# Gate and up projections by one Strassen step: seven half-block products, gone through product by product over a group of pairs

## The chip, the cores and the metric

The kernel runs on one core of one Trainium2 chip. The metric is the device time of one execution in microseconds. Engines are named PE (TensorE), DVE (VectorE), ACT (ScalarE), POOL (GpSimd) and SP (SyncE, which issues most DMAs).

## The reference, cut to what matters

The model is a two-layer decoder trunk over 1088 tokens (1024 prompt tokens and 64 sample tokens), width 1024, hidden width 2816, all in float32. Each layer has an attention part and then this feed-forward part; only the feed-forward part is changed.

```
def rms_norm(x, g):
    y = x * lax.rsqrt(jnp.mean(x * x, axis=-1, keepdims=True) + EPS)
    return y * g

def swiglu(x, w_gu, w_dn):
    gate, up = jnp.split(x @ w_gu, 2, axis=-1)      # w_gu: 1024 x 5632
    return (jax.nn.silu(gate) * up) @ w_dn          # w_dn: 2816 x 1024

xp = xp + swiglu(rms_norm(xp, g_ffn[l]), w_gate_up[l], w_down[l])
```

## The kernel before, in words

Everything is kept transposed: features on the 128 partitions, the 1088 tokens along the free axis. The width 1024 is 8 blocks of 128 rows. To get float32 accuracy from the fast float32r matmul, every operand is split into a rounded part ("high", `WH`, `XH`) and the rest ("low", `WL`, `XL`), and a product is three passes: high by high, high by low, low by high. The high part is a copy on ACT, the low part a subtraction on DVE.

A weight matrix comes in slabs of 128 output columns. One slab (`slab`, L1478) is 8 row blocks times 3 passes times 3 column chunks of 384, 384 and 320 tokens (`CH`), 72 matmuls, accumulated in three banks of the on-chip accumulator PSUM. Two slabs are in flight (`j` = 0 and 1): banks 0 to 2 and banks 3 to 5.

The hidden width is 22 blocks of 128. They are gone through in four groups of 6, 6, 5 and 5 (`FCH`, L44). For each group, the phase `gu` runs pairs of slabs, first the gate slab, then the up slab of the same hidden block; then the phase `dn` multiplies the group's hidden blocks by their rows of `w_down`, in 8 slabs, and adds to the residual `XT`. The order on every engine is written out by hand (`t_phase` on ACT L641, DVE L981, PE L1494; `ffn` on ACT L816, DVE L1221, PE L1765), with counting semaphores between engines; PE's phases are hardware loops.

Per gate/up slab the stations are: SP loads 512 KB into one half of `RAW` (L355, once the former slab's high and low parts are made), POOL multiplies it by the norm's gain (`scale`, L488 to L499), ACT makes `WH` (`split_hi`, L630 to L639), DVE makes `WL` (`split_lo`, L976 to L979), PE multiplies. Per pair, DVE multiplies the gate's sums by the reciprocal root mean square `RB` into `GT`, ACT applies silu, DVE multiplies by `RB` again (L1234), then by the up sums from PSUM (L1239); ACT makes the high part `HH` (L828), DVE the low part `HL` (L1242). POOL does nothing else in the feed-forward part. At the start of a layer's feed-forward part, `after_o` (L669, L1204) makes `XH` and `XL` of the residual, `sums` (L1511) sums squares with a matmul by ones, and `roots` and `rstd` turn them to `RB`.

`copies` (L233) sends two DRAM-to-DRAM copies of 2032 KB each (the cache outputs) down SP's queue, once in each of the eight groups, after the group's fourth gate/up slab.

## Time and profile before

| | |
|---|---|
| time, median of 3 runs | 2522.32 us (2521.43 to 2523.72) |
| profiled execution, first to last instruction | 2520.1 us; its time outside this span is not recorded |
| PE matmul busy | 2429.5 us, 96% |
| DVE / ACT / POOL busy | 999.8 (40%) / 673.0 (27%) / 373.8 us (15%) |
| mean granted PE clock | 0.989 of full |
| DMA | 186.65 MB, mean 74 GB/s |
| first feed-forward part | about 409 to 1172 us from the span's start |
| second feed-forward part | about 1724 to 2496 us |

In the slices of the page (40 of 63 us each) PE stands at 9 tenths in nearly all; the exceptions are the attention part of the first layer (slices 1 to 4), that of the second (slices 22 to 27), and the end. In the feed-forward slices DVE is at 2 to 3 tenths, ACT at 1, POOL at 1 or 0.

### The profile page before, as it was taken

Reading aid. Unit: us, or ns where it says so; the run is one execution under the profiler, and the core shown is the slowest. Engines: PE = TensorE matmul, PEld = TensorE weight load, DVE = VectorE, ACT = ScalarE, POOL = GpSimd, SP = SyncE. Lnnn points to the kernel's source line nnn. Section 1 sums busy time; section 2 is a strip of 40 time slices with the busy share of each in tenths; the row PEclk is TensorE's granted clock in tenths of the full one; section 3 lists DMA queues with packets and bytes.
Section 4 is the critical chain, followed back from the end, with each engine's and each line's share of the span. In section 5 each row is a group of like instructions: output and inputs, shape, how many; then the busy total and the mean of one; then the engine's idle time right before and its main releaser. Section 6 shows DMA issues by size and latency. Waiting matters only on the chain. (4 is left out here: it accounts for less than half of the span.)

```text
span 2520.1 us, 40445 instructions
## 1 busy us (share of the span) xinstructions
PE 2429.5 (96%) x16347; PEld 2343.7 (93%) x16347; DVE 999.8 (40%) x1883; ACT 673.0 (27%) x1283; POOL 373.8 (15%) x282
## 2 busy tenths in 40 slices
PE   8999899999999999999999998789999999999997
PEld 7888699999999999999999976489999999999997
DVE  6466535332322332335312377556322332232235
ACT  4345424211111111113110187443311110111123
POOL 2333201101100100101111110511101100101100
PEclk9999999999999999999999999899999999999998
DMA  4010214113111311311121234713113111312212
GB/s 176 21 54 20 87 51 133 48 37 113 50 35 48 116 33 51 108 38 54 63 85 49 72 92 138 263 53 113 47 38 114 44 40 50 108 38 67 95 35 87
DMA packets 64939, 186.65 MB, mean 74 GB/s; under 512 B 11288, under 2 KB 17816, under 8 KB 64056
## 3 DMA queue, kind: packets, MB, share of 16 engines
q1 hardware_dynamic: 63928, 180.46, 22.0%
q0 software_dynamic: 912, 4.85, 0.5%
q8 instruction: 65, 1.06, 0.2%
q14 instruction: 34, 0.28, 0.0%
HBM read 175.85 MB, written 44.70 MB: 88 GB/s over the span
## 5 line engine op out<-in xcount | busy, mean ns | idle before, releaser
L978 DVE TENSOR_TENSOR WL<-RAW,WH 128x1024 fp32r<-128x1024 f32 (+3 forms) x196 | 220.0, 1124 | 1137.3 <-ACT WH L639 1136.6
L1488 PE MATMUL PS<-XH,WH 128*128 128x384 f32 x2640 | 582.5, 328 | 2.8 <-DVE XL L1005 1.6
L1488 PE MATMUL PS<-XL,WH 128*128 128x384 f32 x2640 | 581.7, 328 | 0.0
L1488 PE MATMUL PS<-XH,WL 128*128 128x384 f32 x2640 | 581.7, 328 | 0.0
L639 ACT CAST WH<-RAW 128x1024 fp32r<-128x1024 f32 (+3 forms) x196 | 184.8, 944 | 1154.0 <-PE PS L1488 1137.7
L498 POOL TENSOR_TENSOR RAW<-RAW,GAIN 128x1024 f32<-128x1024 f32 x112 | 217.1, 1940 | 1636.9 <-DMA RAW<-in_w_gu 1383.0
L1488 PEld LDWEIGHTS PS<-XH,WH 128*128 128x128 f32 x2640 | 450.5, 188 | 3.9 <-DVE XL L1005 1.9
L1488 PEld LDWEIGHTS PS<-XH,WL 128*128 128x128 f32 x2640 | 450.6, 188 | 0.0
L1488 PEld LDWEIGHTS PS<-XL,WH 128*128 128x128 f32 x2640 | 450.6, 188 | 0.0
L1488 PE MATMUL PS<-HL,WH 128*128 128x384 f32 (+1 forms) x1041 | 228.7, 327 | 0.0
L1488 PE MATMUL PS<-HH,WL 128*128 128x384 f32 (+1 forms) x1041 | 228.5, 327 | 0.0
L1488 PE MATMUL PS<-HH,WH 128*128 128x384 f32 (+1 forms) x1041 | 228.5, 327 | 0.0
L1488 PEld LDWEIGHTS PS<-HH,WL 128*128 128x128 f32 x1041 | 176.0, 188 | 0.0
L1488 PEld LDWEIGHTS PS<-HH,WH 128*128 128x128 f32 x1041 | 176.0, 188 | 0.0
L1488 PEld LDWEIGHTS PS<-HL,WH 128*128 128x128 f32 x1041 | 175.9, 188 | 0.0
L1188 DVE TENSOR_TENSOR XT<-XT,PS 128x768 f32 (+3 forms) x158 | 106.2, 713 | 3.5 <-PE PS L1488 3.4
L537 POOL TENSOR_TENSOR SA<-SA,SM 128x512 f32<-128x512 f32 (+1 forms) x64 | 72.3, 1131 | 129.3 <-DVE SM L1104 129.3
L732 ACT ACTIVATE SA<-SA,SM 128x257 f32<-128x257 f32 (+1 forms) x128 | 62.6, 491 | 99.8 <-DVE SM L1095 99.8
L857 ACT ACTIVATE SB<-SB,ST 128x128 f32<-128x128 f32 (+1 forms) x192 | 84.3, 446 | 8.8 <-DVE ST L1287 8.8
L1242 DVE TENSOR_TENSOR HL<-HT,HH 128x1088 f32 (+1 forms) x44 | 56.9, 1292 | 59.0 <-ACT HH L828 59.0
L828 ACT CAST HH<-HT 128x1088 f32 (+1 forms) x44 | 48.6, 1104 | 112.9 <-DVE HT L1239 112.9
L1234 DVE TENSOR_TENSOR GT<-GT,RB 128x1088 f32<-128x1088 f32 x44 | 56.9, 1292 | 52.0 <-ACT GT L824 52.0
(235 smaller groups left out, 2443.5 us busy)
## 6 DMA issues: line engine op xcount, KB each, us to landing
RAW<-in_w_gu SPq DMA_DIRECT2D x88, 512.0 KB, 3.6
out_bkS<-in_bk_in SPq DMA_DIRECT2D x8, 2032.0 KB
out_bvS<-in_bv_in SPq DMA_DIRECT2D x8, 2032.0 KB
RAW<-in_w_dn SPq DMA_DIRECT2D x32, 384.0 KB, 3.0
KC<-in_bk_in SPq DMA_DIRECT2D x8, 1536.0 KB, 11.5
VC<-in_bv_in SPq DMA_DIRECT2D x8, 1536.0 KB, 6.9
RAW<-in_w_dn SPq DMA_DIRECT2D x32, 320.0 KB, 2.9
XT<-in_xT SPq DMA_DIRECT2D x16, 544.0 KB, 5.4
```

Of the source, the lines that this page charges most:

```text
L498: nc.gpsimd.tensor_tensor(w, w, g, ALU.mult).then_inc(S["scaled"], 1)
L537: nc.gpsimd.tensor_tensor(p, p, SM[:, 24 + 2 * b:26 + 2 * b].unsqueeze(2).to_broadcast([P, 2, w]), ALU.mult).then_inc(S["a_norm"], 1)
L639: nc.scalar.copy(to[:, j, 0:nk * P], RAW[:, j, 0:nk * P]).then_inc(S["wh"], 1)
L732: ins = nc.scalar.activation(SA[:, b, kk, 256 - w:257], SA[:, b, kk, 256 - w:257], ACT.Exp, bias=SM[:, h:h + 1], scale=-1.0, accum_out=SM[ ...
L828: nc.scalar.copy(HH[:, ds(i * TOK, TOK)], HT[:]).then_inc(S["hh"], 1)
L857: ins = nc.scalar.activation(s, s, ACT.Exp, bias=ST[:, g, blk, 2 * p + kk:2 * p + kk + 1], scale=-1.0, accum_out=ST[:, g, blk, 8 + 2 * p + ...
L978: nc.vector.tensor_tensor(lo[:, j, 0:nk * P], RAW[:, j, 0:nk * P], hi[:, j, 0:nk * P].bitcast(F32), ALU.subtract).then_inc(S["wl"], 1)
L1188: ins = nc.vector.tensor_tensor(x, x, ps, ALU.add)
L1234: nc.vector.tensor_tensor(GT[:], GT[:], RB[:], ALU.mult).then_inc(S["gt"], 1)
L1242: nc.vector.tensor_tensor(HL[:, ds(i * TOK, TOK)], HT[:], HH[:, ds(i * TOK, TOK)].bitcast(F32), ALU.subtract).then_inc(S["hx"], 1)
L1488: ins = mm(PS[:, 3 * j + c, 0:width], w[:, j, k * P:(k + 1) * P], x(k, a, width), start=(k == 0 and n == 0), stop=(k == nk - 1 and n == 2))
```

## The change: what it does

The block matrix product is done by Strassen's scheme once. Tokens are cut into two halves of 544, the width 1024 into two halves of 4 blocks, and the output columns of a pair into gate and up. With X(ij) the half blocks of the activations (i: rows 0 to 3 or 4 to 7 of the width, j: token half) and W the four quarter slabs of a pair (gate or up, upper or lower rows), seven products of half size replace eight. A product is 4 row blocks times 3 passes times 2 chunks of 272 tokens, 24 matmuls, in two PSUM banks.

In each group of n pairs the program goes through product 0 for all n pairs, then product 1, and so on: seven phases of n products ("g" counts them, 0 to 7n-1, phase = g // n). What each phase needs and leaves, beside its matmuls:

| phase | weights summed on POOL | activations summed on POOL | PSUM copies on ACT | PSUM adds on DVE |
|---|---|---|---|---|
| 0 | yes | no | 2 | 0 |
| 1 | no | yes | 1 | 1 |
| 2 | yes | no | 1 | 1 |
| 3 | no | yes | 0 | 2 |
| 4 | yes | yes | 0 | 2 |
| 5 | yes | yes | 0 | 1 |
| 6 | yes | yes | 0 | 1 |

The results are accumulated in on-chip memory: `GA` and `UA`, two halves of 544 for each pair. The sums of activations go to `TS` in four pieces per phase, and their high and low parts to `TH` and `TL` (double buffered by phase). The gain is now multiplied into the activations by ACT (`gained`, into `XG`), so POOL's `scale` over the gate/up weights goes. The weight ring has four places instead of two. Both multiplications of the gate by `RB` move from DVE to POOL (`gate_rms`), before and after silu: one half of the tokens during phases 3 and 4, the other during phases 5 and 6. The product with up, and `HH` and `HL`, are made per token half (`hidden`, `hidden_low`), in phases 5 and 6 and just behind. The down projection keeps its matmuls. Most of the diff is the bookkeeping of semaphore counts and buffers; below is its core, first the constants, then POOL's functions, DVE's `ffn` and PE's `product`. The loops over the feed-forward part are written out; the cache copies are issued at the second slab of the down phase.

```diff
 FCH = (6, 6, 5, 5)
+HALF = TOK // 2
+CHK = HALF // 2
+NPH = 7
+PAIRED = (0, 2, 4, 5, 6)
+SUMMED = (1, 3, 4, 5, 6)
+COPIES = (2, 1, 1, 0, 0, 0, 0)
+ADDS = (0, 1, 1, 2, 2, 1, 1)
...
+            def weight_sum(l, c, g):
...
+                pool.wait_ge(S[f"raw{r}"], 16 * n)
+                one, two = ring(r)[:, 0:4 * P], ring(r)[:, 4 * P:KT * P]
+                if ph < 5:
+                    ins = nc.gpsimd.tensor_tensor(one, one, two, ALU.add)
...
+            def operand_sum(l, c, ph, k):
...
+                pool.wait_ge(S["slab"], operand_free(l, c, ph))
...
+                nc.gpsimd.tensor_tensor(TS[operand_slot(l, c, ph)][:, k * HALF:(k + 1) * HALF], one, two, op).then_inc(S["ts"], 1)
+            def gate_rms(l, c, i, h, again):
...
+                    pool.wait_ge(S["gad"], evicted(ADDS, l, c, (5, 3)[h] * FCH[c] + i))
...
+                nc.gpsimd.tensor_tensor(g, g, RB[:, h * HALF:(h + 1) * HALF], ALU.mult).then_inc(S[f"g{h + 1}{'m' if again else 'r'}"], 1)
+            def ffn(l):
+                for g in range(4):
+                    weight_sum(l, 0, g)
+                for c, n in enumerate(FCH):
+                    for g in range(NPH * n):
+                        ph, i = divmod(g, n)
+                        for h, at in ((1, 3), (0, 5)):
+                            if 0 <= g - 3 - at * n < n:
+                                gate_rms(l, c, g - 3 - at * n, h, True)
+                        if g + 4 < NPH * n:
+                            weight_sum(l, c, g + 4)
+                        for h, at in ((1, 3), (0, 5)):
+                            if 0 <= g - 2 - at * n < n:
+                                gate_rms(l, c, g - 2 - at * n, h, False)
+                        if i < 4 and ph + 1 in SUMMED and (ph or c == 0):
+                            operand_sum(l, c, ph + 1, i)
+                    if c + 1 < len(FCH):
+                        for k in range(4):
+                            operand_sum(l, c + 1, 1, k)
+                        for g in range(4):
+                            weight_sum(l, c + 1, g)
...
             def ffn(l):
...
+                    for g in range(NPH * n):
+                        ph, i = divmod(g, n)
+                        if g:
+                            product_adds(l, c, g - 1)
...
+                        if g + 3 < NPH * n:
+                            gate_up_low(l, c, g + 3)
...
+                        if 0 <= g - 1 - 6 * n:
+                            hidden(l, c, g - 1 - 6 * n, 1)
+                        if 1 <= i < 5 and ph + 1 < NPH and (ph or c == 0):
+                            operand_low(l, c, ph + 1, i - 1)
...
+                        if 0 <= g - 4 - 5 * n < n:
+                            hidden(l, c, g - 4 - 5 * n, 0)
+                        if 0 <= g - 5 - 5 * n < n:
+                            hidden_low(l, c, g - 5 - 5 * n, 0)
+                        if 0 <= g - 2 - 6 * n:
+                            hidden_low(l, c, g - 2 - 6 * n, 1)
+                    product_adds(l, c, NPH * n - 1)
+                    hidden(l, c, n - 1, 1)
+                    hidden_low(l, c, n - 2, 1)
+                    hidden_low(l, c, n - 1, 1)
...
+            def product(l, c, g):
...
+                pe.wait_ge(S["wl"], PLAN.first[f"gu{l}{c}"] + g + 1)
+                if g >= 3:
+                    pe.wait_ge(S["gcp"], evicted(COPIES, l, c, g - 3))
+                    if evicted(ADDS, l, c, g - 3):
+                        pe.wait_ge(S["gad"], evicted(ADDS, l, c, g - 3))
...
+                for k in range(4):
+                    if i == 0:
+                        pe.wait_ge(S["tl"], piece(l, c, ph, k))
+                    for n, (w, x) in enumerate(((wh, TH[q]), (wh, TL[q]), (wl, TH[q]))):
+                        for d in range(2):
+                            a = k * HALF + d * CHK
+                            ins = mm(PS[:, b + d, 0:CHK], w[:, k * P:(k + 1) * P], x[:, a:a + CHK],
+                                     start=(k == 0 and n == 0), stop=(k == 3 and n == 2))
```

## Rows read from the trace of the kernel before

**Rows 1.** The page: span, and part 1, busy us of each engine.
```profile
span 2520.1 us, 40445 instructions
PE 2429.5 (96%) x16347; PEld 2343.7 (93%) x16347; DVE 999.8 (40%) x1883; ACT 673.0 (27%) x1283; POOL 373.8 (15%) x282
```
**Rows 2.** Windows over the feed-forward parts: length, busy of each engine, clock, DMA, GB/s.
```profile
409.00:937.00 528.00, 528.00 (x3175) 527.92 (x3174) 163.58 (x179) 96.54 (x93) 59.36 (x31) 1.00 0.22 70
...
1724.00:2496.00 772.00, 772.00 (x4643) 771.93 (x4642) 243.13 (x276) 144.55 (x142) 76.31 (x40) 1.00 0.19 60
```
**Rows 3.** PE's waits, the longest: us in total, times, longest.
```profile
PE PS L1862 <- ACT CB L914: 19.3, 7, 4.2
```
**Rows 4.** Timeline of PE in a gate/up slab: start us, us, instruction, count.
```profile
702.16 0.66 PE L1488 MATMUL PS<-XH,WL 128*128 128x384 f32 x3
...
706.66 0.66 PE L1488 MATMUL PS<-XH,WL 128*128 128x384 f32 x3
```
**Rows 5.** The line of 256-column matmuls: ns min/median/max, first and last start.
```profile
L1538 PE MATMUL PS<-WHV,XH x72: 279/281/357, 42.0 to 67.5; 128*128 128x256 f32 x72
...
L1538 PE MATMUL PS<-WLV,XH x72: 274/281/285, 42.2 to 67.7; 128*128 128x256 f32 x72
```
**Rows 6.** DVE groups by shape: count, busy us, mean ns, idle before.
```profile
L1234 DVE TENSOR_TENSOR GT<-GT,RB 128x1088 f32<-128x1088 f32 x44 | 56.9, 1292 | 52.0 <-ACT GT L824 52.0
L1188 DVE TENSOR_TENSOR XT<-XT,PS 128x768 f32 x52 | 49.2, 947 | 0.0
L978 DVE TENSOR_TENSOR WL<-RAW,WH 128x640 fp32r<-128x640 f32 x32 | 26.4, 825 | 161.0 <-ACT WH L639 161.0
L1188 DVE TENSOR_TENSOR XT<-XT,PS 128x320 f32 x52 | 25.0, 480 | 0.0
L1023 DVE RECIPROCAL RB<-RB 128x384 f32<-128x384 f32 x8 | 19.9, 2524 | 10.0 <-ACT RB L684 10.0
```
**Rows 7.** One line of DVE, four instructions of 512 columns: ns min/median/max.
```profile
L1035 DVE TENSOR_TENSOR WL<-RAW,WH x4: 679/691/1522, 5.7 to 15.1; 128x512 fp32r<-128x512 f32 x4
```
**Rows 8.** POOL groups by shape.
```profile
L537 POOL TENSOR_TENSOR SA<-SA,SM 128x512 f32<-128x512 f32 x56 | 67.2, 1202 | 100.4 <-DVE SM L1104 100.3
L587 POOL TENSOR_TENSOR QB<-QB 128x512 f32<-128x512 f32 x16 | 24.5, 1534 | 33.5 <-DVE QB L1357 30.9 <-issue 2.2 <-POOL SQN L578 0.2
L594 POOL TENSOR_TENSOR PSB<-PSB 128x256 f32<-128x256 f32 x8 | 5.8, 727 | 9.8 <-ACT PSB L881 9.3
L596 POOL TENSOR_TENSOR PSB<-PSB 128x64 f32<-128x64 f32 x8 | 2.5, 318 | 0.0
```
**Rows 9.** Timeline of DVE from 1193 us.
```profile
1193.45 1.29 DVE L1017 TENSOR_TENSOR SQS<-SQS,SQ 128x1088 f32<-128x1088 f32 x1
1194.65 2.99 DVE L1005 TENSOR_TENSOR XL<-XT,XH 128x1088 fp32r<-128x1088 f32 x1
```
**Rows 10.** Timeline of POOL in the same stretch.
```profile
1193.68 2.82 POOL L498 TENSOR_TENSOR RAW<-RAW,GAIN 128x1024 f32<-128x1024 f32 x1 [5.49 <-DMA RAW<-in_w_kB]
```
**Rows 11.** Timelines of DVE and of POOL at 99.5 us.
```profile
99.54 0.47 DVE L1095 CUSTOM_DVE_ANT_0 SA<-PS,TABA,NSINK 128x256 f32<-128x256 f32 x1
...
98.56 1.04 POOL L537 TENSOR_TENSOR SA<-SA,SM 128x512 f32<-128x512 f32 x1 [1.70 <-DVE SM L1104]
99.56 1.90 POOL L520 TENSOR_TENSOR RAW<-RAW,GAIN 128x1024 f32<-128x1024 f32 x1
```
**Rows 12.** ACT group of the weight copies of 512 columns.
```profile
L639 ACT CAST WH<-RAW 128x512 fp32r<-128x512 f32 x8 | 4.9, 620 | 10.9 <-PE PS L1488 10.8
```
**Rows 13.** Windows over two attention stretches, columns as in Rows 2.
```profile
1580.00:1660.00 80.00, 60.43 (x888) 39.20 (x886) 45.53 (x100) 38.83 (x88) 41.97 (x59) 0.84 0.56 199
280.00:290.00 10.00, 7.42 (x126) 5.87 (x122) 5.17 (x17) 6.59 (x16) 2.04 (x2) 1.00 0.19 57
```
**Rows 14.** SP's queue at the first cache copies, and DMA issues with us to landing.
```profile
408.23 15.65 SPq L239 DMA_DIRECT2D out_avS<-in_av_in  x1
RAW<-in_w_gu SPq DMA_DIRECT2D x88, 512.0 KB, 3.6
```

More of the change, by code:

```diff
@@ L75, in __init__ @@
             self.scaled[name] = z
-            z += n if name[:2] not in ("oA", "oB", "dn") else 0
-            g += 0 if name[0] == "v" else n // 2
+            z += n if name[:2] not in ("oA", "oB", "dn", "gu") else 0
+            g += 0 if name[0] == "v" or name[:2] == "gu" else n // 2
+            self.raw[name] = tuple(raw[:2])
+            if name[:2] in ("gu", "dn"):
+                first = self.first[f"gu{name[2]}0"]
+                for x in range(n):
+                    r = (self.first[name] + x - first) % 4
+                    raw[r] += 2 if name[:2] == "gu" and x * NPH // n == 4 else 1
+                    self.ring[name, x] = r, raw[r]
+            else:
+                raw[0] += n // 2
+                raw[1] += n // 2
     def end(self, name):
@@ L542, in _ @@
                     scale_one("qA", 4 + U // 8, 0)
-            for c in range(len(FCH)):
-                scale(f"gu0{c}", 1)
+            def weight_sum(l, c, g):
+                ph = g // FCH[c]
+                if ph not in PAIRED:
+                    return
+                r, n = PLAN.ring[f"gu{l}{c}", g]
+                pool.wait_ge(S[f"raw{r}"], 16 * n)
+                one, two = ring(r)[:, 0:4 * P], ring(r)[:, 4 * P:KT * P]
+                if ph < 5:
+                    ins = nc.gpsimd.tensor_tensor(one, one, two, ALU.add)
+                elif ph == 5:
+                    ins = nc.gpsimd.tensor_tensor(one, one, two, ALU.subtract)
+                else:
+                    ins = nc.gpsimd.tensor_tensor(one, two, one, ALU.subtract)
+                ins.then_inc(S["gsum"], 1)
@@ L647, in pair @@
                             split_hi(name, 2 * i + j + 2, j)
-                        elif prefetch and PLAN.next(name) and not (j and name == "oA"):
+                        elif ahead and j == 0:
+                            ahead()
+                        elif prefetch and PLAN.next(name) and not ahead:
                             split_hi(PLAN.next(name), j, j)
@@ L801, in evac @@
                     k = 2 * i + j
-                    if not split and isinstance(k, int) and k == KT - 1:
+                    if norm in (1, 4) and isinstance(k, int) and k == KT - 1:
                         return
@@ new lines, in down_low, with first_jobs, ahead @@
+            def down_low(l, c, x):
+                r, _ = PLAN.ring[f"dn{l}{c}", x]
+                dve.wait_ge(S["wh"], PLAN.first[f"dn{l}{c}"] + x + 1)
+                nc.vector.tensor_tensor(down_slot(WL, c, x), ring(r)[:, 0:FCH[c] * P], down_slot(WH, c, x).bitcast(F32),
+                                        ALU.subtract).then_inc(S["wl"], 1)
+            def first_jobs(l):
+                def ahead():
+                    if l:
+                        for k in range(4):
+                            operand_low(l, 0, 0, k)
+                    for g in range(2):
+                        gate_up_low(l, 0, g)
+                return ahead
@@ new lines, in down @@
+            def down(l, c, x):
+                n, b = FCH[c], down_bank(c, x)
+                pe.wait_ge(S["wl"], PLAN.first[f"dn{l}{c}"] + x + 1)
+                if x < 2:
+                    pe.wait_ge(S["gad"], evicted(ADDS, l, c, NPH * n - 2 + x))
+                else:
+                    pe.wait_ge(S[f"free{x % 2}"], PLAN.groups[f"dn{l}{c}"] + x // 2)
+                wh, wl = down_slot(WH, c, x), down_slot(WL, c, x)
+                for k in range(n):
+                    if x == 0:
+                        pe.wait_ge(S["hl1"], pairs_ahead(l, c) + k + 1)
+                        pe.wait_ge(S["hl2"], pairs_ahead(l, c) + k + 1)
+                    for m, (w, h) in enumerate(((wh, HH), (wh, HL), (wl, HH))):
+                        for d, (a, width) in enumerate(CH):
+                            ins = mm(PS[:, b + d, 0:width], w[:, k * P:(k + 1) * P], h[:, k * TOK + a:k * TOK + a + width],
+                                     start=(k == 0 and m == 0), stop=(k == n - 1 and m == 2))
+                ins.then_inc(S["slab"], 1)
@@ L1771, in _ @@
+            def ffn(l):
+                for c, n in enumerate(FCH):
+                    for g in range(NPH * n):
+                        product(l, c, g)
+                        if c == 0 and g == n:
+                            norm_sums(1 + 2 * l, (0, 1))
+                        if c == 0 and g == n + 2:
+                            norm_sums(1 + 2 * l, (2,))
+                    for x in range(KT - 1 if (l, c) == (1, len(FCH) - 1) else KT):
+                        down(l, c, x)
             ffn(0)
```

463 lines of the change are left out of this document (356 added, 107 removed).

## The prediction

> **What bounds the kernel now.** I read the page's busy times first: PE is busy 96% of a span of 2520.1 us, no other engine over 40% [rows 1]. Then windows over the feed-forward parts, to see whether the idle 4% lies there: it does not. In 528, 235 and 772 us PE is busy in every microsecond at full granted clock (1.00, the level of 2.4 GHz), DVE 31 to 34% and POOL 9 to 11% of the time [rows 2]. The list of PE's waits agrees: the longest, 19.3 us, stands on a line of the attention part [rows 3]. So the part that changes is bound by PE alone, and two things decide: how much PE work goes, and whether the work that Strassen hands to the lightly used DVE and POOL still fits beside what is left.
>
> **PE's side.** Before, a pass over one row block is three matmuls, 1088 columns; nine passes after 702.16 us the same pass starts at 706.66: 4.50 / 9 = 0.500 us [rows 4], 166.7 ns a matmul of 363 columns. A pair takes 2 x 8 x 3 x 0.500 = 24.0 us, a group of 5 pairs 120 us, of 6 pairs 144 us. After, a pair is 7 x 24 = 168 matmuls of 272 columns. No row has that width. The nearest has 256: 216 matmuls start between 42.0 and 67.7 us, 25.7 / 215 = 119.5 ns each [rows 5]. Interpolated to 272 with the slope to 363 columns, (166.7 - 119.5) / 107 = 0.44 ns a column, it is 126.5 ns; bounds are 119.5 and 141.7 ns (three quarters of 166.7 by columns would be 125, plus one whole 16.7 ns if all of the width step were fixed cost). A product is then 24 x 0.1265 = 3.04 us, a pair 21.3 us, a group 106.3 (n=5) or 127.5 us (n=6). If PE remained the bound, 4 x (13.7 + 16.5) = 121 us would go.
>
> **The others' side.** Prices. DVE with both inputs in on-chip memory: 1292 ns for 1088 columns, 825 for 640 [rows 6], 679 to 691 for 512 when undisturbed [rows 7]; so 0.69 us for a weight low (512 columns), 0.725 for 544 columns (operand low, hidden, hidden low). DVE with one input in PSUM: 947 at 768, 480 at 320 [rows 6], so 0.71 us for 544. POOL with two full inputs: 727 ns at 256 columns and 318 at 64 [rows 8], a slope of 2.13 ns a column: 1.27 us for a weight sum (512), 1.34 for 544 columns (operand sum, gate_rms). The bounds for 512 columns are 1.04 us (the 1202 ns row, whose second input is two values repeated; 1.04 is its undisturbed time, as its first timeline entries show and 1202 is with waits) and 1.53 us (the strided adds of L587) [rows 8]. I take 1.27, since it comes from contiguous operands like these.
>
> The price that decides is another: DVE and POOL exclude each other. At 1193.68 POOL is given a scaling of 1.90 us while DVE is in a subtraction (end 1194.74); it ends at 1196.50, so it began only when DVE was through. DVE's next operation, issued at 1194.65, takes 2.99 us instead of 1.28 and ends 1.14 us behind POOL's end [rows 9, 10]. One POOL and one DVE operation thus take 2.99 us where their own times add to 3.18: strictly one after the other, less 0.19 us of overlap at the change. An operation of DVE that reads PSUM is not held: 0.47 us as usual under a running POOL multiplication [rows 11]. So product_adds run freely, but every weight low, operand low, hidden and hidden low shares one resource with every POOL operation; I call it the shared path.
>
> Now count the shared path by phase, from the loops in the diff (n=5, a group that is not a layer's first):
>
> - phase 0: DVE 6, POOL 1: 5.4 us; phase 1: 9 and 4: 11.4 us; phase 2: 9 and 5: 13.0 us. PE needs 15.2 us for each, and DVE's adds (5 x 0.71) run beside POOL: PE stays the bound, 45.6 us in all.
> - phase 3: DVE 5 weight lows, 4 operand lows, 6.4 us; POOL 4 weight sums, 5 gate_rms, 4 operand sums, 17.1 us: 23.5 us.
> - phase 4: DVE 6.4; POOL 5 + 5 + 4, 18.4: 24.8 us.
> - phase 5: DVE 7.1; POOL 5 + 5 + 4, 18.4: 25.5 us.
> - phase 6 with its tail: DVE 2 weight lows, 1 down low (0.82), 19 hidden operations, 16.0; POOL 1 + 5, 8.0: 24.0 us.
>
> Phases 3 to 6: 97.7 us on the shared path against 4 x 15.2 = 60.8 us on PE. For n=6 the same count gives 26.9 + 26.7 + 31.6 + 27.5 = 112.7 us against 73.0; phases 0 to 2 take PE's 54.7.
>
> From these I take off the overlaps at the changes: 34 alternations (the smaller count of each phase) x 0.19 and 1.7 us for back-to-back operations, 97.7 - 8.5 = 89.2 us; for n=6, 40 x 0.19 and 1.8: 112.7 - 9.8 = 102.9 us (with no overlap at all, 97.7 and 112.7, the high bound).
>
> Can the queues shift work out of phases 3 to 6? POOL is in order: operand sums of phase ph+1 wait until PE is through phase ph-1, gate_rms waits for DVE's adds of two products ago, and the weight sums stand between them. The 29 us that the shared path idles in phases 0 to 2 cannot be used. PE can only be some 3 products ahead (its banks wait for the adds of product g-3). Forward, the tail can overlap: the first down slab takes its hidden blocks one by one, 1.5 us each (nine matmuls), so I take off 3 us for hidden operations beside PE; and add 1.5 us in phase 6, where POOL runs out of work before DVE and DVE's five adds of 0.71 no longer hide. Net 1.5 us off; bounds 0 and 6 off.
>
> Group of 5: 45.6 + 89.2 - 1.5 = 133.3 us against 120: +13.3. Group of 6: 54.7 + 102.9 - 1.5 = 156.1 against 144: +12.1. Four of each: +101.6 us.
>
> **The remaining edits.** ACT per product: a weight high 0.62 us [rows 12], up to two PSUM copies of about that, pieces of 544 at half of 1115 ns plus start; under 2 us of 3.04, hidden. The norm's reciprocals (7 us of DVE, phase 1 of a layer's first group) fit: DVE has 18.2 us there for 11.4 of its own. That group also gets its phase-1 operand sums and lows in phase 0, 8.3 us on top of 7.4 in 18.2: fits. A layer's start needs 4 operand pieces instead of 8: -3 to +5 us, taken as 0. Each product now loads up to 512 KB; a load lands in 3.6 us [rows 14] with four ring places, about seven products ahead: hidden. The cache copies keep SP busy for 15.65 us [rows 14] and now stand ahead of the third down slab's load, issued some six products before the down phase; that slab is needed 6 x 3.04 + 15 = 33 us later: hidden; if not, up to 10 us in each of eight groups.
>
> **Rule against row.** The only two-input POOL rows are short or strided. The Trainium skill (GPSIMD Engine Reference, section 3.1) puts a two-input elementwise operation at about 2.6 cycles an element at 1.2 GHz, since both operands come through one port; that would be 1.11 us plus dispatch for 512 columns, nearer 1.27 than 1.04, and speaks against the change: the sum by it is the one above, by the cheap row it would be the third case below.
>
> **Sum.** 2520.1 + 101.6 = 2621.7 us of span. The median lies 2.2 us above the span, so 2624 us.
>
> **Rivals.**
> (a) Forecast: shared path binds phases 3 to 6. Own range 2580 to 2690 (no overlap: +70 us; 6 us off: -36 us).
> (b) Faster: PE stays the bound because POOL and DVE together stay under 3.04 us a product. Price: 121 us off, 2401 us, perhaps 2410 with starts. It decides where the shared path of phases 3 to 6 is below 60.8 us (n=5). For it: DVE at 33% and POOL at 10% now, ring and banks several deep. Against it: POOL's own 62 us in those phases already exceed 60.8 even if DVE were never in the way. Chance 0.13.
> (c) POOL runs at the cheap price, 1.04 and 1.11 us: 10.8 us less (n=5), 12.5 (n=6), 93 in all: 2531 us. For it the repeated-operand rows, against it the 727/318 pair. Chance 0.12.
> (d) Dearer: PE idles about a third of phases 3 to 6, and its clock may fall. With 76% busy it was granted 0.84 on average, a mix of the 1.2 and 2.4 GHz levels, but 1.00 with 74% elsewhere [rows 13]. A product at 1.2 GHz takes 24 x 272 / 1200 + 0.32 = 5.76 us; all of phases 3 to 6 so: 115 against 89, 138 against 103, in all +245: 2869. A mean clock of 0.84 still carries 68% busy, so the forecast has 0 for it. The strided POOL price gives +114, 2738. Chance 0.17.
> (a) keeps 0.58.
>
> **Numbers.** Range 2500 to 2740: leaves out (b), and the far end of (d). What can be told from no change is about 0.2%, 5 us. Faster 0.17 ((b) and the low part of (c)), within 0.04, slower 0.79.
>
> **What would show it.** After: POOL busy near 900 us instead of 374, with mean durations of its 544-column operations well above 1.34 and DVE's two-input ones above 0.73, while the PSUM adds stay at 0.71. Windows by phase: PE at 100% in phases 0 to 2 and the down phases, near 70% in phases 3 to 6, n products taking 22 to 26 us. Products in phases 0 to 2 at 3.04 us show the matmul price. It would be wrong if POOL and DVE ran side by side, if the matmul pitch at 272 columns were over 135 ns, or if PE's waits in these parts were for loads or PSUM copies instead of WL, TL and HL.

## The result and the profile after

The changed kernel takes 2682.39 us (median of 4 runs, 2681.75 to 2683.32), the kernel before 2523.02 us (2521.43 to 2524.16) beside it: ratio 1.0635, 95% interval 1.0622 to 1.0648. It is 6.35% slower. The profiled execution of the changed kernel has a span of 2680.5 us, 160.4 us more than before [rows 1], at a mean granted clock of 0.954 of full.

The page of the changed kernel, span and busy us of each engine:

```profile
span 2680.5 us, 43596 instructions
PE 2390.0 (89%) x17403; PEld 2285.7 (85%) x17403; DVE 1599.0 (60%) x2575; ACT 969.6 (36%) x1973; POOL 1088.5 (41%) x750
```

PE is recorded busy for 39.5 us less than before [rows 1], not for the 121 us less that were forecast: part of its work now runs at a fallen clock and takes longer (in x1 below, at a mean granted clock of 0.987, the same matmuls keep it busy for 2302.9 us, 127 us less than before). It stands idle for 290 us instead of 91. DVE went from 1000 to 1599 us, POOL from 374 to 1088: these are recorded durations, and the next rows show that they hold waiting. The groups of POOL and of DVE in the changed kernel (count, then busy us, mean ns of one, then idle time before them):

```profile
L726 POOL TENSOR_TENSOR GA<-GA,RB 128x544 f32<-128x544 f32 x176 | 287.5, 1635 | 44.7 <-ACT GA L1082 44.7
L715 POOL TENSOR_TENSOR TS<-XG 128x544 f32<-128x544 f32 x160 | 255.5, 1608 | 125.0 <-PE PS L2197 119.4 <-ACT XG L879 5.6
L700 POOL TENSOR_TENSOR RAW<-RAW 128x512 f32<-128x512 f32 x66 | 97.2, 1473 | 389.1 <-DMA RAW<-in_w_gu 389.1
```
```profile
L1519 DVE TENSOR_TENSOR TL<-TS,TH 128x544 fp32r<-128x544 f32 x160 | 222.1, 1388 | 5.2 <-ACT TH L893 1.8
L1583 DVE TENSOR_TENSOR UA<-UA,GA 128x544 f32<-128x544 f32 x88 | 109.1, 1262 | 2.5
L1576 DVE TENSOR_TENSOR UA<-UA,PS 128x544 f32<-128x544 f32 x88 | 62.2, 707 | 0.0
```

An operand low takes 1388 ns on average where it needs 720, a product with up 1262. The addition with an input in PSUM, of the same 544 columns, stays at 707 ns. That is the picture of rows 9 to 11, now in every group: who reads two operands from on-chip memory takes turns with POOL, who reads PSUM does not.

PE's waits in the changed kernel, the longest (us in total, times, longest):

```profile
PE PS L2197 <- DVE UA L1576: 76.7, 45, 3.0
PE PS L2197 <- DVE TL L1519: 43.2, 23, 3.7
PE PS L2216 <- issue: 27.2, 4, 7.1
PE PS L2216 <- DVE WL L1531: 26.1, 4, 7.7
PE PS L2197 <- DVE GA L1574: 23.3, 12, 4.1
PE PS L2321 <- ACT CB L1220: 19.3, 7, 4.2
```

Before, the longest was the last of these [rows 3]; now five stand ahead of it, 196.5 us, all in the feed-forward part. Three are the products' (L2197), for DVE's additions and lows; two are the first down slab's (L2216). None is a load or a copy by ACT. The largest part, 100.0 us, is for the additions from PSUM (L1576 and L1574). They are not slower than before, they come late: DVE works through its queue in order, and they stand in it behind operations that POOL holds up.

Windows over the second group of 6 pairs in the first layer (phases 0 to 2, phases 3 to 6, the down phase) and over its last group of 5 (phases 0 to 2, phases 3 to 6; columns as in rows 2: length, busy of PE, PE's weight loads, DVE, ACT, POOL, then granted clock, DMA share, GB/s):

```profile
636.50:690.50 54.00, 54.00 (x433) 54.00 (x432) 30.36 (x40) 27.83 (x50) 14.69 (x10) 1.00 0.39 118
690.70:798.70 108.00, 79.99 (x579) 77.09 (x577) 91.61 (x90) 34.40 (x57) 93.67 (x58) 0.94 0.45 145
798.70:872.20 73.50, 73.50 (x432) 73.50 (x433) 26.28 (x37) 12.57 (x19) 6.88 (x6) 0.97 0.18 56
1071.60:1116.60 45.00, 45.00 (x361) 45.00 (x361) 24.16 (x35) 23.93 (x43) 12.77 (x9) 1.00 0.40 124
1116.70:1204.90 88.20, 67.75 (x482) 65.81 (x480) 71.41 (x75) 29.61 (x49) 75.84 (x47) 0.91 0.46 146
```

In phases 0 to 2 PE is busy in every microsecond at full clock, 54.0 and 45.0 us. In phases 3 to 6 PE's 72 and 60 us of matmuls take 108.0 and 88.2. DVE and POOL are each recorded busy for 81 to 87% of that stretch; where one of DVE's instructions with both inputs in on-chip memory or one of POOL's is under way (the union of their records, worked out from the trace) it is 102.4 of 108.0 and 84.2 of 88.2 us.

Where the 160.4 us lie, from the first matmuls of each phase in the trace. Eight groups, four of each size:

| stretch | PE's minimum forecast | forecast | measured |
|---|---|---|---|
| phases 0 to 2 | 401 | 401 | 396.8, and 6.6 more in phase 0 of the two first groups |
| phases 3 to 6, n=5 | 243 | 351 | 360.7 (92.1, 88.3, 92.0, 88.3) |
| phases 3 to 6, n=6 | 292 | 406 | 432.4 (108.2, 108.0, 108.2, 108.0) |
| gate and up, sum (before: 1056) | 936 | 1158 | 1196.5 |
| down phases, over before | 0 | 0 | +17.4 (+1.9 to +2.4 each) |
| all else | 0 | 0 | +2.5 |

1196.5 - 1056 + 17.4 + 2.5 = 160.4 us. The sums of squares by PE in the first groups (two matmul groups, about 2 us a layer) are in both kernels and left out of the rows.

### The profile page after: what moved, and what is told of

Read it like the earlier page. It is cut to its first block and busy times, and to the rows that moved or that the text cites. A ratio compares the mean times of both kernels' runs of the same rounds, so it can differ in the third digit from the quotient of the medians.

```text
span 2680.5 us, 43596 instructions
## 1 busy us (share of the span) xinstructions
PE 2390.0 (89%) x17403; PEld 2285.7 (85%) x17403; DVE 1599.0 (60%) x2575; ACT 969.6 (36%) x1973; POOL 1088.5 (41%) x750
## 5 line engine op out<-in xcount | busy, mean ns | idle before, releaser
L2197 PE MATMUL PS<-TH,WH 128*128 128x272 f32 x2464 | 538.1, 301 | 149.4 <-DVE UA L1576 76.7
L2197 PEld LDWEIGHTS PS<-TH,WH 128*128 128x128 f32 x2464 | 406.3, 198 | 167.8 <-issue 115.4
L2197 PE MATMUL PS<-TH,WL 128*128 128x272 f32 x2464 | 527.8, 297 | 0.0
L2197 PE MATMUL PS<-TL,WH 128*128 128x272 f32 x2464 | 525.5, 296 | 0.0
L2197 PEld LDWEIGHTS PS<-TL,WH 128*128 128x128 f32 x2464 | 405.1, 197 | 0.0
L2197 PEld LDWEIGHTS PS<-TH,WL 128*128 128x128 f32 x2464 | 402.9, 197 | 0.0
L715 POOL TENSOR_TENSOR TS<-XG 128x544 f32<-128x544 f32 x160 | 255.5, 1608 | 125.0 <-PE PS L2197 119.4
L726 POOL TENSOR_TENSOR GA<-GA,RB 128x544 f32<-128x544 f32 x176 | 287.5, 1635 | 44.7 <-ACT GA L1082 44.7
L2216 PE MATMUL PS<-HH,WH 128*128 128x384 f32 (+1 forms) x1041 | 236.9, 337 | 53.3 <-issue 27.2
L2216 PE MATMUL PS<-HL,WH 128*128 128x384 f32 (+1 forms) x1041 | 234.7, 334 | 0.0
L2216 PE MATMUL PS<-HH,WL 128*128 128x384 f32 (+1 forms) x1041 | 232.6, 332 | 0.0
L2216 PEld LDWEIGHTS PS<-HH,WH 128*128 128x128 f32 x1041 | 181.7, 194 | 54.9 <-issue 27.9
L1519 DVE TENSOR_TENSOR TL<-TS,TH 128x544 fp32r<-128x544 f32 x160 | 222.1, 1388 | 5.2 <-ACT TH L893 1.8
L1525 DVE TENSOR_TENSOR WL<-RAW,WH 128x512 fp32r<-128x512 f32 x156 | 140.5, 904 | 108.0 <-ACT WH L903 107.9
L2216 PEld LDWEIGHTS PS<-HL,WH 128*128 128x128 f32 x1041 | 182.2, 194 | 0.0
L2216 PEld LDWEIGHTS PS<-HH,WL 128*128 128x128 f32 x1041 | 180.1, 192 | 0.0
L646 POOL TENSOR_TENSOR RAW<-RAW,GAIN 128x1024 f32<-128x1024 f32 x24 | 58.6, 2447 | 215.9 <-DMA RAW<-in_w_qB 89.8
```

The costliest lines, as they stand in the source:

```text
L646: nc.gpsimd.tensor_tensor(w, w, g, ALU.mult).then_inc(S["scaled"], 1)
L715: nc.gpsimd.tensor_tensor(TS[operand_slot(l, c, ph)][:, k * HALF:(k + 1) * HALF], one, two, op).then_inc(S["ts"], 1)
L726: nc.gpsimd.tensor_tensor(g, g, RB[:, h * HALF:(h + 1) * HALF], ALU.mult).then_inc(S[f"g{h + 1}{'m' if again else 'r'}"], 1)
L1519: nc.vector.tensor_tensor(TL[q][:, a:b], x, TH[q][:, a:b].bitcast(F32), ALU.subtract).then_inc(S["tl"], 1)
L1525: nc.vector.tensor_tensor(slot(WL, c, g), ring(r)[:, 0:4 * P], slot(WH, c, g).bitcast(F32), ALU.subtract).then_inc(S["wl"], 1)
L2197: ins = mm(PS[:, b + d, 0:CHK], w[:, k * P:(k + 1) * P], x[:, a:a + CHK], start=(k == 0 and n == 0), stop=(k == 3 and n == 2))
```

## The experiments

Each run is compared with runs of the kernel before on the same chip. The medians of the kernel before on these chips are 2521.6 to 2524.5 us, so some 3 us between two runs from different chips mean nothing. x1 and x2 ran once, the others four or five times. Theory A is that of the prediction: the shared path of DVE and POOL bounds phases 3 to 6. The letters B to H are its rivals, as each expectation states them.

### x1_pool_stub: POOL's work in the feed-forward part cut to one column

```diff
-                one, two = ring(r)[:, 0:4 * P], ring(r)[:, 4 * P:KT * P]
+                one, two = ring(r)[:, 0:1], ring(r)[:, 4 * P:4 * P + 1]
...
-                nc.gpsimd.tensor_tensor(g, g, RB[:, h * HALF:(h + 1) * HALF], ALU.mult)
+                nc.gpsimd.tensor_tensor(g[:, 0:1], g[:, 0:1], RB[:, h * HALF:h * HALF + 1], ALU.mult)
```

The operand sums are cut in the same way, and the lows read `XG` instead of their result.

> The changed kernel with every POOL operation of the feed-forward parts (weight sums, operand sums, both gate multiplications) cut to one column, all waits and all work of the other engines kept; so the sums are left out of the result. Theory A (DVE's two-input operations and POOL's operations take turns on one shared path, and that path bounds phases 3 to 6): with POOL's 70 to 85 us a group gone, PE is the bound except at the tail, where DVE's own 19 hidden operations and the adds of phase 6 (about 19 us against 15) still stand over; groups of about 108 (n=5) and 129 us (n=6), the whole 2420 to 2450 us. DVE's 544-column two-input operations go back to 0.72 us from 1.26 to 1.39. Rival B (DVE is late by itself, or loads and PSUM copies are late): DVE keeps its work, so at least half of the 160 us stays, 2600 us or more. Rival C (the granted clock of PE does it): clock returns to 0.99 with the idle gone, so C alone doesn't part from A here.

Measured: 2403.27 us (one run), against 2524.45 before. A group takes 128 to 131 and 106 us, PE's own 126.3 and 105.3, the down phases are back at 71.6 (one: 73.1) and 59.7 to 59.9. All instructions of all engines are still there (43596). The groups of DVE in this kernel:

```profile
L1519 DVE TENSOR_TENSOR TL<-XG,TH 128x544 fp32r<-128x544 f32 x224 | 160.1, 719 | 6.7 <-ACT TH L893 6.7
L1525 DVE TENSOR_TENSOR WL<-RAW,WH 128x512 fp32r<-128x512 f32 x156 | 106.7, 687 | 60.1 <-ACT WH L903 60.1
...
L1576 DVE TENSOR_TENSOR UA<-UA,PS 128x544 f32<-128x544 f32 x88 | 62.9, 714 | 0.0
L1583 DVE TENSOR_TENSOR UA<-UA,GA 128x544 f32<-128x544 f32 x88 | 61.4, 721 | 2.5
```

The operand low falls from 1388 to 719 ns, the product with up from 1262 to 721, the PSUM addition stays. So the columns that POOL works on account for 2682.4 - 2403.3 = 279 us, and with them gone the change brings the 121 us that PE alone was forecast to save: nothing else in it (waits, copies, loads, turnover of banks) costs PE more than the 2 us at the end of a group of 6. It is the time of rival (b), 2401 us, and 17 us under the lower end expected here; why A's estimate was that much too high was not looked into. x1 alone does not say whether POOL's columns cost by holding DVE or by POOL's own queue being full; x5 does.

### x2_rms_stub: only the gate's multiplications cut to one column

```diff
-                nc.gpsimd.tensor_tensor(g, g, RB[:, h * HALF:(h + 1) * HALF], ALU.mult)
+                nc.gpsimd.tensor_tensor(g[:, 0:1], g[:, 0:1], RB[:, h * HALF:h * HALF + 1], ALU.mult)
```

> The changed kernel with only the two gate multiplications on POOL cut to one column (the gate is not normalised in the result). Theory A: 20 (n=5) or 24 (n=6) operations of 1.34 us leave the shared path of phases 3 to 6, which falls to about 65 and 74 us against PE's 60 and 72; with 3 us of tail a group takes about 114 and 132 us, the whole about 2480 to 2505 us, some 180 to 200 us less than the changed kernel. Rival B (DVE alone, its operations and adds, or the loads): under 40 us less.

Measured: 2492.06 us (one run), in A's range. 176 multiplications of 1.35 us are 238 us; leaving them out gives 190 us. Groups go from 162.1 to 137.1 (the second) and from 133.4 to 111.4 us (the last): phases 4 and 5 now run at PE's 18.0 and 15.0 to 15.6, and only phase 6 is late (28.9 and 20.6). The multiplications are the largest part, but what is left of POOL's work still delays phase 6, which takes 20.1 and 15.6 us in x1.

### x3_late_sums: the next group's operand sums wait for the down phase

```diff
                     if c + 1 < len(FCH):
+                        pool.wait_ge(S["slab"], PLAN.first[f"dn{l}{c}"] + 1)
                         for k in range(4):
                             operand_sum(l, c + 1, 1, k)
```

> The changed kernel, complete, with one more wait on POOL: the four operand sums for the next group (and the weight sums behind them) start only when the first down slab is through, not when the last product is. In the trace these four POOL operations alternate with DVE's last three hidden operations, which the first down slab waits for. Theory A: they cost what the last group of each layer, which has no such sums, does without: 137.1 - 133.4 = 3.7 us in each of six groups, so 18 to 26 us less than the changed kernel. Rival D (the tail is bound by the chain DVE, ACT, DVE alone): no change, within 4 us.

Measured: 2654.76 us (2653.61 to 2657.49), ratio 1.0523 (1.0505 to 1.0540), 27.6 us less than the changed kernel. Behind phase 6 the changed kernel's POOL starts the four sums of the next group at once, and three of DVE's last hidden operations (the product with up, L1583, and its low, L1589) alternate with them. The first down slab does not wait for these three themselves, as the expectation has it, but for what stands behind them in DVE's queue: here the addition that ends at 2194.92. The changed kernel, POOL, then DVE, then PE's first matmul of the down phase:

```profile
2179.48 1.35 POOL L726 TENSOR_TENSOR GA<-GA,RB 128x544 f32<-128x544 f32 x1 [1.89 <-ACT GA L1082]
2188.56 6.92 POOL L715 TENSOR_TENSOR TS<-XG 128x544 f32<-128x544 f32 x4 [7.73 <-PE PS L2197]
```
```profile
2182.58 1.35 DVE L1589 TENSOR_TENSOR HL<-UA,HH 128x544 fp32r<-128x544 f32 x2
...
2188.02 0.96 DVE L1531 TENSOR_TENSOR WL<-RAW,WH 128x768 fp32r<-128x768 f32 x1
2188.89 1.85 DVE L1583 TENSOR_TENSOR UA<-UA,GA 128x544 f32<-128x544 f32 x1
2190.67 3.62 DVE L1589 TENSOR_TENSOR HL<-UA,HH 128x544 fp32r<-128x544 f32 x2
2194.21 0.71 DVE L1576 TENSOR_TENSOR UA<-UA,PS 128x544 f32<-128x544 f32 x1
```
```profile
2195.02 1.25 PE L2216 MATMUL PS<-HH,WH 128*128 128x384 f32 x3 [6.54 <-issue]
```

The program has PE wait there until the addition of the last product but one has emptied its bank, and in all four groups of 6 the down phase starts 0.1 us behind that addition. In the groups of 5 it starts 0.1 us behind the first weight low of the down phase (L1531), which stands behind the same addition in DVE's queue.

With the sums held back, DVE in the same place of the second group:

```profile
789.64 0.72 DVE L1584 TENSOR_TENSOR UA<-UA,GA 128x544 f32<-128x544 f32 x1
790.28 1.35 DVE L1590 TENSOR_TENSOR HL<-UA,HH 128x544 fp32r<-128x544 f32 x2
```

Two lows take 1.35 us with POOL idle and 3.62 beside it. In each layer the three groups that have a successor gain 3.4 to 4.0 us each, 22 us in all, and the last one nothing (133.4 to 133.3). In the profiled executions, 28.3 us apart, the down phases give 2.7 us, and the rest lies outside the feed-forward parts, where this edit changes nothing. This is a term that the prediction did not have.

### x4_warm: eight more matmuls in each product of phases 4 to 6

```diff
+                    for e in range(8 if k == 0 and ph >= 4 else 0):
+                        mm(PS[:, b + e % 2, 0:CHK], wh[:, 0:P], TH[q][:, 0:CHK], start=True, stop=True)
```

> The changed kernel, complete, with eight more matmuls of 272 columns at the head of each product of phases 4 to 6 (overwritten by the product's first pass, so nothing changes in the result): 1.0 us of PE work in stretches where PE idles 5 to 18 us a phase. Theory A: the shared path sets the pace there, so the extra 8 x 15 to 18 us a group cost nothing; what changes is the granted clock, which fell to 1.2 GHz for 10 to 17 us in each group: part of it comes back, and with it at most the 2 us by which each down phase was longer and some of the tail, 0 to 20 us less in all (2660 to 2685). Rival C (the clock is the cause of the loss): 40 us less or more. Rival E (PE is nearly the bound in these phases): 60 to 120 us more.

Measured: 2673.88 us (2672.34 to 2678.37), ratio 1.0601 (1.0583 to 1.0618), 8 us less than the changed kernel with 1056 matmuls more. The extra ones are 1056 x 0.1253 = 132 us of PE. The same stretch as above, phases 3 to 6 of the second group, now runs at the full clock:

```profile
690.00:796.00 106.00, 91.38 (x717) 89.84 (x715) 88.76 (x89) 33.98 (x57) 91.94 (x57) 1.00 0.43 147
```

Its clock is 1.00 instead of 0.94, and phases 3 to 6 take 106.8 us instead of 108.0. Over phases 3 to 6 of all groups the granted clock stands at 0.50 for 38 us instead of 138, and yet these phases take 790.2 us instead of 793.1 in the profiled executions. So PE has slack there that 132 us of work fit into, and the fallen clock costs about 3 us there, since it falls where PE waits anyway. The other 5 of the 8 us are not traced to it: the profiled execution is the slowest of the four. At the start of the down phases the clock still falls, to 0.50 for 3.2 to 6.2 us in every group, and they take as long as in the changed kernel (535.1 and 534.6 us in all); x4 does not price that.

### x5_rms_dve: the gate's multiplications on DVE

```diff
-                nc.gpsimd.tensor_tensor(g, g, RB[:, h * HALF:(h + 1) * HALF], ALU.mult)
+                nc.vector.tensor_tensor(g, g, RB[:, h * HALF:(h + 1) * HALF], ALU.mult)
```

The calls move from POOL's loop to DVE's, behind `product_adds`, in the same order.

> The changed kernel, complete, with both gate multiplications issued by DVE at the same places of its queue instead of by POOL. Theory A: the same work stays on the shared path, but at 0.725 us each instead of 1.35, so phases 3 to 6 lose 12.3 (n=5) and 14.8 us (n=6), less some overlap: about 80 to 110 us less in all, 2575 to 2600 us. Rival F (POOL's queue alone is the bound, DVE and POOL run side by side): POOL falls from 62 to 35 us in phases 3 to 6, DVE's own 72 us minus its 9 us of overlaps is then the longest, 63 against 88 us now: 180 to 200 us less. Rival B (DVE alone is the bound): 14.5 to 17.4 us more of DVE work a group, 100 us slower.

Measured: 2622.33 us (2619.47 to 2625.93), ratio 1.0395 (1.0377 to 1.0412): 60 us less than the changed kernel. The direction is A's, and F and B fell, but A's own size, 80 to 110 us, was missed. The window over phases 3 to 6 of the second group tells why:

```profile
685.90:787.90 102.00, 80.54 (x580) 78.56 (x578) 98.74 (x114) 33.29 (x57) 56.77 (x34) 0.92 0.46 154
```

DVE is recorded busy for 98.7 of 102.0 us, POOL for 56.8, and the union of the shared instructions is 88.6. The shared path now has 13 us free, but DVE has not: it also carries the PSUM additions, and whenever POOL is in the way the whole queue of DVE stands. A reading that fits is a second bound beside the shared path: DVE's own work plus the work of POOL that it is blocked by.

### x6_norm_first: activations normalised once, no multiplication of the gate

The residual times gain (`XG`, 8 blocks of 1088 columns) is multiplied by `RB` before the first product, so that gate and up come out normalised and `gate_rms` goes. The late sums of x3 are in.

```diff
+            def normalise(l, k):
+                dve.wait_ge(S["xg"], KT * l + k + 1)
+                x = XG[:, ds(k, 1)].rearrange("p a h n -> p (a h n)")
+                nc.vector.tensor_tensor(x, x, RB[:], ALU.mult).then_inc(S["xr"], 1)
...
-                                gate_rms(l, c, g - 3 - at * n, h, True)
...
-                                gate_rms(l, c, g - 2 - at * n, h, False)
```

> A complete kernel: the changed kernel, but the activations are multiplied by the reciprocal root mean square before the first product (eight DVE operations of 1088 columns a layer), so both gate multiplications go; the sums of squares, roots and reciprocals move ahead of the first product; and the wait of the experiment with late sums is in. Theory A: phases 3 to 6 have about 65 and 74 us on the shared path against 60 and 72 on PE, groups of about 112 and 130 us, first groups without the reciprocals in them; the two layer starts now wait some 14 us each for the chain square, sum, root, three reciprocals, multiplication. In all 2520 + 8 x (121 - 132) + 28 + 7 = 2467, between 2450 and 2500 us: faster than the kernel before. Rival B (DVE bound): 2600 us or more.

Measured: 2515.17 us (2510.69 to 2519.11), ratio 0.9969 (0.9953 to 0.9984), 15 us above the expected range. The groups that do not start a layer came near what A says, 133.0 to 133.6 us (about 130 expected) and 110.8 to 112.3 (about 112). What was underrated is the layer's start. DVE there:

```profile
402.37 6.98 DVE L1313 RECIPROCAL RB<-RB 128x384 f32<-128x384 f32 x3 [2.35 <-ACT RB L906]
409.38 2.49 DVE L1534 TENSOR_TENSOR XG<-XG,RB 128x1088 f32<-128x1088 f32 x2
...
416.90 7.13 DVE L1534 TENSOR_TENSOR XG<-XG,RB 128x1088 f32<-128x1088 f32 x4
423.95 3.57 DVE L1507 TENSOR_TENSOR WL<-GR,WH 128x512 fp32r<-128x512 f32 x2
```

Three reciprocals (7.0 us) and the multiplications stand ahead of the first operand low, so the first product starts at 412.7 us instead of 394.7, and phase 0 takes 27.9 us where PE needs 18.0: 28 us in the first layer against PE's pace. Against the changed kernel, whose phases 0 and 1 take 22.0 and 19.9 us, it is 22 us. PE waits there, and it also runs slower: the mean granted clock of this phase 0 is 0.78.

### x7_norm_wdve: x6, and the weight sums of phases 5 and 6 on DVE

```diff
+            def late_weight_sum(l, c, g):
...
+                nc.vector.tensor_tensor(one, a, b, ALU.subtract).then_inc(S["gsd"], 1)
...
+                        if g + 4 < NPH * n:
+                            late_weight_sum(l, c, g + 4)
```

> A complete kernel: the one with normalised activations, with the weight sums of phases 5 and 6 (2n a group) issued by DVE four products ahead instead of by POOL: 0.69 us instead of 1.27 on the shared path. Its groups now take 112 and 133 us where PE alone needs 105 and 126. Theory A: 9 to 11 operations less long on the path, 5 to 6 us a group, of which the part up to PE's own time can come: 1 to 3 us a group, 10 to 25 us less than the kernel with normalised activations (2490 to 2505). Rival G (these groups are now bound by DVE's own work in phases 4 to 6, which rises by 7 us): 0 to 40 us more.

Measured: 2496.35 us (2493.40 to 2500.17), ratio 0.9898 (0.9881 to 0.9916): 19 us less than x6, in A's range, and 1.0% faster than the kernel before. A weight sum costs the shared path 0.69 us on DVE and 1.28 on POOL. A's account of where the gain lies is only half borne out. In the profiled executions, 14.0 us apart, gate and up take 995.8 us instead of 1001.0 and the down phases 526.3 instead of 530.7; the other 4.4 us lie outside the feed-forward parts. The groups of 6 that do not start a layer gain 1.5 and 2.1 us, but three of the four groups of 5 take 114 us instead of 111 to 112: their phase 5 takes 21.0 us instead of 15.4 to 16.7, which is what rival G says. PE's longest waits that are left in this kernel's feed-forward part:

```profile
PE PS L2198 <- DVE TL L1497: 33.6, 9, 8.6
...
PE PS L2217 <- issue: 14.7, 4, 3.7
...
PE PS L2169 <- DVE SQS L1302: 9.4, 2, 5.0
PE PS L2198 <- DVE WL L1514: 6.6, 2, 3.9
```

L2169 is the matmul for the sums of squares at a layer's start.

### x8_recip: the reciprocals of the feed-forward norms cut to one column

```diff
+                    if norm in (1, 3):
+                        w = 1
                     nc.vector.reciprocal(RB[:, a:a + w], RB[:, a:a + w]).then_inc(S["rb"], 1)
```

> The changed kernel with the reciprocals of the feed-forward norms cut to one column (the rest of RB is left as the root, so the gate is scaled by other numbers). In the changed kernel phases 0 and 1 of a layer's first group take 22.0 and 19.9 us, those of the second group of 6 pairs 18.0 each. Theory A: the four or five reciprocals of 2.4 us, in DVE's order between the lows that PE needs, are the cause; without them both first groups lose 5 to 6 us, phases 0 and 1 come to 18 to 19 us, and the time is 10 to 12 us under the changed kernel's 2682 (2669 to 2675). Rival G: the first group's extra operand sums on POOL are the cause; then the time stays within 3 us of 2682 and the phases as they are.

Measured: 2683.01 us (2681.38 to 2683.32), ratio 1.0642 (1.0624 to 1.0660): no gain. My reading fell. Phase 1 of the two first groups still takes 19.9 us; the 1.9 us over 18.0 are PE's own matmuls for the sums of squares, which the kernel before has too. Phase 0 takes 20.4 us in the first layer (22.0 in the changed kernel) and 20.6 in the second (20.6). The 1.6 us less do not come from the reciprocals: x4, which keeps them, shows 20.4 too, and the reciprocals stand in phase 1. G is not tested by a run of its own, but the trace supports it for phase 0, where the second product waits 2.15 us for a weight low that alternates with operand sums on POOL. This kernel's DVE and POOL in that place:

```profile
402.69 3.58 DVE L1527 TENSOR_TENSOR WL<-GR,WH 128x512 fp32r<-128x512 f32 x2
```
```profile
400.25 5.48 POOL L715 TENSOR_TENSOR TS<-XG 128x544 f32<-128x544 f32 x3
```

### x9_split: x7 with every second weight sum of phase 5 back on POOL

```diff
+def summed_late(c, g):
+    ph, i = divmod(g, FCH[c])
+    return ph == 6 or (ph == 5 and i % 2 == 1)
```

> The version with the activations normalised first and the weight sums of phases 5 and 6 on DVE, but with every second weight sum of phase 5 back on POOL. There, DVE's own count in phase 4 of a group of 5 is 10 adds x 0.71 + 5 weight lows x 0.69 + 4 operand lows x 0.725 + up to 5 weight sums x 0.69 = 16.9 us against PE's 15.0, and phase 5 took 21.0 us. Theory A (each phase costs the largest of three sums: PE's, DVE's own, and the shared path): moving two of the five back gives DVE 15.5 us and the shared path about 16.5; the groups of 5 lose 1 to 4 us each, the time is 5 to 15 us less than 2496, 2481 to 2491. Rival H: the shared path alone counts, each sum moved back adds 1.27 - 0.69 us: 5 to 10 us more, 2501 to 2506.

Measured: 2499.54 us (2492.63 to 2505.88), ratio 0.9913 (0.9886 to 0.9940), not told apart from x7. A's 5 to 15 us less fell (phase 5 still takes 20.8 to 21.0 us in three of the four groups of 5); H's 5 to 10 more is not shown either. DVE ahead of phase 5 of the third group:

```profile
910.20 1.19 DVE L1519 TENSOR_TENSOR RAW<-RAW 128x512 f32<-128x512 f32 x1
911.31 1.82 DVE L1525 TENSOR_TENSOR WL<-GR,WH 128x512 fp32r<-128x512 f32 x1
913.05 1.85 DVE L1508 TENSOR_TENSOR TL<-TS,TH 128x544 fp32r<-128x544 f32 x1
914.82 0.71 DVE L1587 TENSOR_TENSOR GA<-GA,PS 128x544 f32<-128x544 f32 x1
```

POOL's four operand sums begin at 910.80 and take 6.62 us, and PE waits 4.00 us for the low that ends at 914.90. DVE's queue is full without a gap from 888 to 919 us. I had added up DVE's own work for the phase (15.5 us) and the shared path (16.5) separately; x5's second bound, DVE's own work plus what blocks it, fits better, since taking a sum off DVE puts a longer one of POOL in its way; that this is the whole reason is argued, not shown.

## Why the prediction was right, and where its sizes were off

**What bounds.** That PE would not stay the bound, and that the exclusion between DVE and POOL would take its place, is shown. (The DVE operation at 1193.45 us in rows 9, which the prediction calls a subtraction, is the addition of squares; it has two inputs in on-chip memory too, and the reading holds.) Durations moved as forecast: POOL's 544-column operations 1608 to 1635 ns on average, DVE's two-input ones 1026 to 1388, the PSUM additions 707. x1 shows that without POOL's columns nothing of the loss is left, x4 that PE has room in the late phases, x5 that moving an operation from POOL to DVE shortens the time although DVE has more to do. Two of the signs came otherwise: POOL is recorded busy for 1089 us, not near 900, and PE's longest waits are for the additions from PSUM, not for WL, TL and HL.

**PE's price.** 126.5 ns a matmul was forecast for 272 columns. The changed kernel, two points of the timeline of PE 108 matmuls apart:

```profile
1801.51 0.41 PE L2197 MATMUL PS<-TL,WH 128*128 128x272 f32 x2
...
1815.04 0.41 PE L2197 MATMUL PS<-TL,WH 128*128 128x272 f32 x2
```

13.53 us / 108 = 125.3 ns, a product 3.007 us instead of 3.04: 4.4 us less in phases 0 to 2 of all groups. Against this sits the layer's start, taken as 0 within -3 to +5: it cost 4.0 and 2.6 us, which the trace of x8 puts down to operand sums and lows in each other's way. The prediction's check there (8.3 us on top of 7.4 in 18.2: fits) added up the work and left out its order.

**Prices of POOL and DVE.** Undisturbed, POOL's 544 columns take 1.35 us (forecast 1.34) and 512 take 1.28 (1.27), DVE's 0.72 (0.725). Rival (c), the cheap price, fell with that. The Trainium skill (GPSIMD Engine Reference, section 3.1) has about 2.6 cycles an element for such an operation, at 1.2 GHz an estimate of 2.17 ns; the two measured times differ by 0.07 us for 32 columns, 2.2 ns a column, and agree with it.

**The shared path's length.** Take the last group of 5 of the first layer, from the first product of phase 3 to the first down matmul: 87.7 us were forecast, 88.3 measured. The terms are all in the trace. The path is under way for 84.3 us of the stretch, and 4.1 us of hidden operations follow beside the first down slab: 88.4 us, where 89.2 were forecast. For the overlap with that slab 3 us were taken off; it is these 4.1. For time in which the path is free and PE waits all the same 1.5 us were added; it is 4.0, three of them in phase 6. For a group of 6 with the next group's sums out of the way (x3, second group) the three terms are 101.7 (forecast 102.9), 3.5 (3) and 5.8 (1.5), in all 104.0 us where 101.4 had been forecast. So the count of the path and the overlap were right within 1.2 us, and the free time was too small by 2.5 to 4.8 us. That the errors nearly cancel for n=5 is luck.

**The step that failed in size** is the end of the group, "phase 6 with its tail", and behind it the sentence that the additions from PSUM "run freely". An addition takes its usual 0.71 us, but it starts late, behind blocked operations in DVE's queue: PE waits 100.0 us for additions in all. At a group's end, all of the first down slab's waits (53.3 us in the eight groups, the two L2216 rows of the waits) stand ahead of its first matmul. What ends them is an addition in the groups of 6 and a weight low in the groups of 5, each behind three or four hidden operations. In six of eight groups the next group's four operand sums, which I had placed beside the down phase, took their turns among these. That collision costs 22 us in gate and up (x3). Without it, phases 3 to 6 are longer than forecast by 12.4 us in the four groups of 6 and by 2.2 in the four of 5, the free time above. These three terms make 37 of the 38.9 us by which gate and up were underestimated.

**How phases shared the load** was forecast wrongly. I expected 22 to 26 us in each of phases 3 to 6; the last group of 5 shows 15.0, 23.1, 21.1 and 29.0. Phase 3 still runs at PE's pace, since the work it consumes was prepared before, and the debt shows one phase later and at the end. The sum is not touched.

**The down phases** were taken as 0 and cost 1.9 to 2.4 us each. They begin at a fallen clock. Windows of the changed kernel over phase 6 and the start of a down phase:

```profile
2168.40:2171.80 3.40, 3.40 (x17) 3.40 (x17) 3.40 (x3) 0.65 (x1) 3.40 (x3) 0.50 0.45 127
...
2192.30:2199.10 6.80, 4.08 (x14) 4.11 (x14) 6.51 (x9) 1.55 (x3) 3.18 (x2) 0.50 0.00 1
2160.00:2168.40 8.40, 3.88 (x29) 3.73 (x30) 6.58 (x6) 3.29 (x6) 6.86 (x5) 1.00 0.16 49
```

Behind 8.4 us with PE busy for 3.88 the granted clock is 0.50, the level of 1.2 GHz, for 3.4 us; it is 0.50 again over the end of the group and the down phase's first 4 us. In each of the eight down phases the clock is 0.50 for the first 4.1 to 5.2 us, and the phase is longer than before by about half of that. In x1, where PE waits at most 1.9 us there, the down phases take 71.6 and 59.7 us, as before, but for one of 73.1 over which the clock fell. Rival (d), a fallen clock over all of phases 3 to 6, did not come: the average in the windows is 0.91 and 0.94, and x4 prices it at about 3 us in these phases. At the low level, from 2180.17 to 2184.70 us, twenty matmuls of 272 columns start, 226.5 ns apart, so a product there takes 5.44 us and not the 5.76 that the rival was priced with.

**The other edits** went as forecast: no wait for a load, for ACT's copies or behind the cache copies stands among PE's waits. The forecast of 2624 us was 58 us short, with the sign and the bound right; a loss of 102 us was forecast, and 159 came. The spans differ by 58.8 us: 38.9 in gate and up (largely the tail), 17.4 in the down phases, 2.5 elsewhere.

**A version that beats both** is x7, 1.0% under the kernel before (0.8 to 1.2%). The change's saving on PE is real (121 us, x1); x7 keeps 25 of it.

## What to carry to other kernels

Before work is moved off PE, add up by phase not each engine's load alone but PE's matmuls against every DVE operation with two on-chip inputs plus every POOL operation. A third sum, DVE's whole queue plus the POOL work that blocks it, was seen full in x5 (98.7 of 102.0 us), but no forecast made with it has been tried, and x9's three separate sums missed. Then go through the in-order queue: an operation that nobody blocks still waits behind one that is blocked. A multiplication that is needed once per hidden block (176 here, 190 us by x2) can cost far more than the same scaling done once on the input (16 longer ones in x6, with 22 us at the first layer's start). Work for the next stage belongs behind the last operation that the current stage's end waits for, even on an idle engine.

## What was not expected of the hardware

- A POOL operation in DVE's way delays all of DVE's queue, the PSUM additions too. In the changed kernel PE's last product starts its last matmul at 2188.19 us; DVE adds the product before it at 2194.21, behind three operations that take 5.5 us beside POOL and 2.1 without it (x3).
- 272 columns cost 125.3 ns a matmul, where 256 cost 119.5 [rows 5] and 363 on average 166.7 [rows 4]: 1088 columns in four matmuls instead of three cost practically the same (125.3 / 272 = 0.461 ns a column against 166.7 / 362.7 = 0.460).
- The granted clock fell to 0.50 in phases 3 to 6 and over the end of every group, and in the down phase it came back while PE was busy without a gap. Filling PE's gaps with matmuls whose results go nowhere cut the time at 0.50 in phases 3 to 6 from 138 to 38 us and these phases by only 3 us (x4).
